# Stick-breaking scores from stacked key parts, half-head value steps, a split last exponential, and a reordered inverse transform

## The reference

```
z = q k^T * 64^-0.5
log_one_minus = where(causal, log_sigmoid(z) - z, 0)
rem = reverse_cumsum(log_one_minus) - log_one_minus
w = where(causal, exp(log_sigmoid(z) + rem), 0)
out = w v
```

## Time and profile before

| | us |
|---|---|
| median of three runs (2299.04 to 2306.05) | 2302.84 |
| profiled execution, its own time | 2304.46 |
| its span in the trace | 2302.7 |
| PE busy | 2166.6 (94%) |
| DVE busy | 1256.4 (55%) |
| ACT busy | 746.9 (32%) |
| POOL busy | 686.1 (30%) |

### The profile page before, as it was taken

The page is one execution under the profiler, slowest core; times in us unless marked ns, Lnnn a source line. Parts: engine busy times, 40 slices in busy tenths (PEclk is TensorE's granted clock), DMA queues, the critical chain, the costliest instruction groups (busy, mean ns, idle before and its releaser), DMA issues. The chain is left out here.

```text
span 2302.7 us, 27418 instructions
## 1 busy us (share of the span) xinstructions
PE 2166.6 (94%) x10821; PEld 1585.2 (69%) x10821; DVE 1256.4 (55%) x2284; ACT 746.9 (32%) x1067; POOL 686.1 (30%) x408
## 2 busy tenths in 40 slices
PE   7859899999999998999999999999999999998988
PEld 6848688888878766778888855436874437885653
DVE  8562389984352066278882032358763563225862
ACT  3422332222142366233232131325651232332210
POOL 6614244445444300344444410011000342441000
PEclk9979899999989999999999989998999979999999
DMA  4032244444423200234443320120002213222102
GB/s 178 7 55 84 72 140 149 141 124 130 131 74 100 83 1 1 82 110 145 148 137 92 92 116 24 55 73 21 2 2 92 92 73 129 92 92 92 74 19 73
DMA packets 51535, 195.49 MB, mean 85 GB/s; under 512 B 9417, under 2 KB 9593, under 8 KB 46191
## 3 DMA queue, kind: packets, MB, share of 16 engines
q1 hardware_dynamic: 37440, 148.53, 20.3%
q0 software_dynamic: 10240, 44.04, 5.5%
q10 hardware_dynamic: 3728, 1.18, 0.3%
HBM read 179.04 MB, written 10.49 MB: 82 GB/s over the span
## 5 line engine op out<-in xcount | busy, mean ns | idle before, releaser
L1474 POOL TENSOR_TENSOR w_lo<-raw,w_hi 128x1024 fp32r<-128x1024 f32 (+1 forms) x216 | 513.7, 2379 | 879.3 <-ACT w_hi L1111 879.2
L586 PE MATMUL psum<-h_hi,w_hi 128*128 128x512 f32 x1216 | 487.9, 401 | 7.7 <-ACT h_hi L1118 5.9
L587 PE MATMUL psum<-h_hi,w_lo 128*128 128x512 f32 x1216 | 480.0, 395 | 0.0
L1111 ACT ACTIVATE w_hi<-raw 128x1024 fp32r<-128x1024 f32 (+1 forms) x216 | 224.9, 1042 | 609.7 <-PE psum L591 399.2
L591 PE MATMUL psum<-h_lo,w_hi 128*128 128x512 f32 x1216 | 303.0, 392 | 0.0
L586 PEld LDWEIGHTS psum<-h_hi,w_hi 128*128 128x128 f32 x1216 | 231.1, 190 | 71.4 <-ACT h_hi L1118 14.4
L591 PEld LDWEIGHTS psum<-h_lo,w_hi 128*128 128x128 f32 x1216 | 230.5, 190 | 48.2
L587 PEld LDWEIGHTS psum<-h_hi,w_lo 128*128 128x128 f32 x1216 | 232.0, 191 | 45.9 <-issue 0.2
L455 PE MATMUL psum<-big,ring 128*128 128x512 f32 x480 | 209.0, 594 | 0.0
L455 PEld LDWEIGHTS psum<-big,ring 128*128 128x128 f32 x480 | 91.0, 191 | 113.8 <-issue 112.7
L633 PE MATMUL psum<-f_hi,w_hi 128*128 128x512 f32 x352 | 137.7, 391 | 0.0
(11 more groups left out here) (374 smaller groups left out, 3326.1 us busy)
## 6 DMA issues: line engine op xcount, KB each, us to landing
raw<-in_ffn_w_up SPq DMA_DIRECT2D x88, 512.0 KB, 3.6
raw<-in_ffn_w_down SPq DMA_DIRECT2D x32, 512.0 KB, 3.6
raw<-in_hy_in SPq DMA_DIRECT2D x32, 512.0 KB, 3.5
ffn_buf<-in_ada_w POOLq DMA_DIRECT2D x20, 512.0 KB, 5.0
sq<-in_ada_w POOLq DMA_DIRECT2D x20, 512.0 KB, 5.0
raw<-in_ssm_w_glu SPq DMA_DIRECT2D x16, 512.0 KB, 3.6
spec<-big SPq DMA_DIRECT2D x8, 1024.0 KB, 3.8
big<-spec POOLq DMA_DIRECT2D x8, 1024.0 KB, 5.1
```

What stands on the lines that cost most here:

```text
L586: pe.matmul(o, hi[:, k, :], h_of(k), start=k == 0, stop=False)
L587: pe.matmul(o, lo[:, k, :], h_of(k), start=False, stop=False)
L1111: act.activation(w_hi[:, (n % 2) * HALF:(n % 2) * HALF + w], raw[:, (n % 4) * HALF:(n % 4) * HALF + w], ACT.Copy).then_inc(S["w_hi"], 1)
L1474: pool.tensor_tensor(w_lo[:, at:at + w], raw[:, (n % 4) * HALF:(n % 4) * HALF + w], w_hi[:, at:at + w].bitcast(F32), ALU.subtract).then_in ...
```

## The change

The keys of a head are now held as a stack: the high part in the head's own 64 partitions, the rest (key minus high part) in the other 64 (`KS`). The queries' high part stands in both halves (`Q_TWICE`), and their rest in `Q_LOW`. A block of scores is one fp32r product over the 128 stacked rows and one fp32r product of the keys' high part with the queries' rest over 64 rows; then the mask as before. ScalarE writes the high parts, VectorE the rests, and GpSimd issues 32 SBUF-to-SBUF DMAs of 128 KB that copy the other halves, between its weight splits; the memsets go. The banks of a head have two keys now, "zA" (blocks 1 to 3) and "zB" (block 0), in this order; the last exponential is in the same two parts, each ahead of the log of that part, and `cum_done` counts three steps per head. `values(t)` is in two steps, block 0 beside head 2t+3 and blocks 1 to 3 beside head 2t+4, both ahead of `cumulate`.

In the Hyena mixer `z_back` runs over the frequency half f outside the four channel blocks and waits for `yw` per half. The last piece, u = 7, is folded, multiplied and summed in two column halves, its fold comes after the sums of u = 6, and `yw` ends at 9.

```diff
-        KZ = bigv(0, 8192).rearrange("p (h t) -> p h t", h=HEADS)
+        KS = f_hi[:, 0:8192].rearrange("p (h t) -> p h t", h=HEADS)
+        K_REST = [v[:, k * L:(k + 1) * L] for v, n in ((f_hi[:, 8192:11264], 6), (f_lo[:, 0:2 * L], 2)) for k in range(n)]
         VT = bigv(8192, 4096).rearrange("p (s n) -> p s n", s=4)
...
+        Q_TWICE = [(HHI, HLO)[h % 2][:, h // 2, :] for h in range(HEADS)]
...
             def scores(h):
...
+                o = z_of(h)
                 if h == 0:
                     pe.wait_ge(S["masks_ready"], 2)
-                    for t in range(8):
-                        pe.wait_ge(*free(("k", t)))
-                        pe.wait_ge(*free(("q", t)))
-                for i in (0, 1, 3, 2):
-                    m = pe.matmul(zblk(o, i), KZ[:, h, i * P:(i + 1) * P], Q[:, h // 2, i * P:L],
-                                  start=i != 3, stop=False, skip_group_check=True)
+                    pe.wait_ge(S["ks_both"], 256)
+                    pe.wait_ge(S["qs_both"], 16 * (HEADS - 2))
+                if h == HEADS - 2:
+                    pe.wait_ge(S["qs_last"], 32)
+                if h % 2 == 0:
+                    pe.wait_ge(*free(("k", h // 2)))
+                    pe.wait_ge(*free(("q", h // 2)))
+                for i in (1, 3, 2, 0):
+                    if i == 1:
+                        take(pe, ("zA", h), bank=3 * (h % 2) + 1, n=2)
+                    if i == 0:
+                        take(pe, ("zB", h), bank=3 * (h % 2))
+                    pe.matmul(zblk(o, i), KS[:, h, i * P:(i + 1) * P], Q_TWICE[h][:, i * P:L], start=i != 3, stop=False,
+                              skip_group_check=True)
+                    m = pe.matmul(zblk(o, i), KS[half(h), h, i * P:(i + 1) * P], Q_LOW[half(h), h // 2, i * P:L],
+                                  start=False, stop=False, skip_group_check=True)
                     m = pe.matmul(zblk(o, i)[:, 0:P], masks[:, 0, :], masks[:, 1, :], start=False, stop=False,
                                   skip_group_check=True)
-                fills(m, key)
+                    if i == 2:
+                        fills(m, ("zA", h))
+                fills(m, ("zB", h))
 
...
                 for ready, sp in ((S["sp_hi"], SPH), (S["sp_lo"], SPL)):
                     pe.wait_ge(ready, 2 * h + 1)
                     for i in (1, 3, 2):
-                        tri(i, sp)
                         later(i, sp)
+                        m = tri(i, sp)
+                m.then_inc(S["cum_done"], 1)
                 pe.wait_ge(S["sp_hi"], 2 * h + 2)
                 later(0, SPH)
                 tri(0, SPH)
-                later(0, SPL)
+                later(0, SPL).then_inc(S["cum_done"], 1)
                 pe.wait_ge(S["sp_lo"], 2 * h + 2)
                 m = pe.matmul(zblk(o, 0), NEGTRI, SPL[:, 0:L], start=False, stop=True, skip_group_check=True)
                 m.then_inc(S["cum_done"], 1)
 
...
-            def values(t):
...
+                o = ps(key) if late else take(pe, key, bank=6 + t % 2)
+                if not late:
+                    for h in (2 * t, 2 * t + 1):
...
+                for i in (1, 2, 3) if late else (0,):
...
                         m = pe.matmul(o[r:r + 64, i * P:L], VT[:, i, h * HD:(h + 1) * HD],
                                       WT[h % 4][:, ZAT[i]:ZAT[i] + L - P * i], start=i == 0, stop=i == 3,
...
+                if late:
+                    fills(m, key)
+
+            for h in range(HEADS + 3):
                 if h < HEADS:
                     scores(h)
+                if h >= 3:
+                    values((h - 3) // 2, h % 2 == 0)
                 if 1 <= h <= HEADS:
                     cumulate(h - 1)
-                if h >= 3 and h % 2:
-                    values((h - 3) // 2)
...
             def z_back(o_, hf):
...
+                keys = [("y", o_, 4 * hf + c) for c in range(4)]
+                for f in range(2):
+                    for c in range(4):
+                        if f == 0:
+                            take(pe, keys[c])
+                        o = ps(keys[c])
+                        if c == 0 or (o_, hf, f, c) == (1, 1, 1, 2):
+                            pe.wait_ge(S["yw"], 2 * (2 * o_ + hf) + f + 1 + c // 2)
+                        for par in range(2):
                             for q, tab in enumerate((INVC, INVS)):
                                 i = pe.matmul(o[:, par * 256:par * 256 + 256], YW[hf][:, f, 2 * q + par, c * P:(c + 1) * P],
-                                              tab[:, f, par * 256:par * 256 + 256], start=f == 0 and q == 0,
-                                              stop=f == 1 and q == 1)
-                    fills(i, key)
+                                              tab[:, f, par * 256:par * 256 + 256], start=f == 0 and q == 0 and par == 0,
+                                              stop=f == 1 and q == 1, skip_group_check=True)
+                        if f:
+                            fills(i, keys[c])
 
...
-                act.wait_ge(S["kz_zero"], t // 2 + 1)
                 act.wait_ge(*full(key))
-                step(act.activation(KZ[0:64, 2 * t, :], ps(key)[0:64, :], ACT.Copy))
-                own()
-                frees(act.activation(KZ[64:128, 2 * t + 1, :], ps(key)[64:128, :], ACT.Copy), key)
+                for h in (2 * t, 2 * t + 1):
+                    act.activation(KS[half(h), h, :], ps(key)[half(h), :], ACT.Copy).then_inc(S["ks_hi"], 1)
...
                 split_hi(HALVES_AT["q"] + t + 2)
-                evac(("q", t), Q[:, t, :], scale=HD ** -0.5)
+                act.wait_ge(*full(("q", t)))
+                for h in (2 * t, 2 * t + 1):
+                    act.activation(Q_TWICE[h][half(h), :], ps(("q", t))[half(h), :], ACT.Copy, scale=HD ** -0.5) \
+                        .then_inc(S["qs_hi"], 1)
...
+                act.wait_ge(*full(("zA", h)))
+                act.wait_ge(*full(("zB", h)))
...
+                own()
+                for q, (lo, hi) in enumerate(SP_PARTS):
+                    if h >= 1:
+                        weights(h - 1, q)
                     act.activation(LN_[b][:, lo:hi], LN_[b][:, lo:hi], ACT.Ln, bias=1.0).then_inc(S["ln_ready"], 1)
...
+            def weights(h, q):
+                act.wait_ge(S["cum_done"], 3 * h + (1, 3)[q])
+                if h >= 4 and q == 0:
                     act.wait_ge(*full(("o", (h - 4) // 2)))
...
+                lo, hi = SP_PARTS[q]
+                z = z_of(h).rearrange("p b n -> p (b n)")[:, lo:hi]
+                frees(act.activation(WT[h % 4][:, lo:hi], z, ACT.Exp), (("zA", "zB")[q], h))
...
+                if t < 8:
+                    split_lo(HALVES_AT["k"] + t + 2)
+                if t:
+                    pool.wait_ge(*free(("k", t - 1)))
+                    for h in (2 * t - 2, 2 * t - 1):
+                        other_half("ks_both", h, KS[:, h, :], K_REST[t - 1])
+            for q in range(7):
+                split_lo(HALVES_AT["v"] + q + 2)
+            for t in range(9):
+                if t < 8:
+                    split_lo(HALVES_AT["q"] + t + 1)
+                if t:
+                    for h in (2 * t - 2, 2 * t - 1):
+                        pool.wait_ge(S["qs_hi"], h + 1)
+                        other_half("qs_both" if t < 8 else "qs_last", h, Q_TWICE[h], Q_TWICE[h])
...
+                for h in (2 * t, 2 * t + 1):
+                    dve.wait_ge(S["ks_hi"], h + 1)
+                    i = TT(K_REST[t][half(h), :], ps(("k", t))[half(h), :], KS[half(h), h, :].bitcast(F32), ALU.subtract)
+                    if h % 2:
+                        frees(i, ("k", t))
+                    else:
+                        step(i)
+                        own()
+            dve.wait_ge(S["ks_both"], 256)
...
+                    i = STT(Q_LOW[half(h), t, :], ps(("q", t))[half(h), :], HD ** -0.5,
+                            Q_TWICE[h][half(h), :].bitcast(F32), ALU.mult, ALU.subtract)
...
                     z_fold(5)
-                after = z_products(u)
-                if u not in (4, 7):
-                    if u != 3:
+                parts = [slice(0, 512)] if u < 7 else [slice(0, 256), slice(256, 512)]
+                for n in parts:
+                    if u == 7:
+                        z_fold(u, n)
+                    after = z_products(u, n)
+                    if u not in (3, 4, 6, 7):
                         z_fold(u + 1)
-                z_sums(u, after)
+                    z_sums(u, after, n)
                 if u == 3:
                     z_fold(4)
...
```

More of the change, by code:

```diff
@@ L714, in cumulate, with values @@
                 m.then_inc(S["cum_done"], 1)
-            def values(t):
-                if t == 0:
+            def values(t, late):
+                if t == 0 and not late:
                     for c in range(2):
@@ L721, in values @@
                 key = ("o", t)
-                o = take(pe, key, bank=6 + t % 2)
-                for h in (2 * t, 2 * t + 1):
```

(44 more changed lines are left out.)

102 lines of the change are left out of this document (41 added, 61 removed).

## The result

The changed kernel takes 2290.47 us (median of four runs, 2288.34 to 2292.03), the kernel before it in the same rounds 2303.52: a ratio of 0.9945, 95% interval 0.9932 to 0.9957. That is 13 us off where 22 were forecast; the time lies in the range. The profiled execution took 2288.34 with a span of 2286.5.

A forecast was written before the change was run, and what follows sets the result against it. The attention loop was taken as bound by TensorE's own list plus a 1.56 us hole in every second head. Loop 18.6 plus Hyena 3.5, about 22 us off 2304.46, gave 2282 us, range 2267 to 2298.

The forecast's parts named there:

- the loop's hole: Attention loop: TensorE's idle 1.56 us in every second head, waiting for ScalarE's last exponential, was forecast to go.
- The list per head: Attention loop: TensorE's work per head, forecast at 6.63 us, or 5.64 plus 9 tile-shape switches.
- the row of another tile shape: Scores: a profiled 33-by-64 product among full ones, showing 0.09 and 0.14 us per switch; 0.11 was taken.
- the third rival: Scores: the array empties at each row-mode switch, 0.35 us each, giving 2315 us; chance 0.06.
- The 13 steps: Attention loop, third head's scores to the last head's: each from 7.69 to 6.63 us, 13.8 us saved.
- The start: Attention loop's beginning: third head's scores no longer wait for all of cumulate and a whole exponential; about 3 us saved.
- The rival of late copies: Before the attention loop: the query DMAs land late, 4.5 us more, giving 2287 us; chance 0.10.
- The tail: Attention's end, last scores to the next projection: from 14.22 to 12.4 us, 1.8 us saved.
- Around the loop: Extra evacuations, VectorE work and DMA issues beside TensorE, and the loop's wait for DMAs: priced at zero.
- a late eighth channel block: Hyena's projection after the last z_back: VectorE is still evacuating, so the eighth channel block costs 0.5 us.
- free switches: Attention loop: tile-shape switches nearly free, 13 x 1.89 us saved there, giving 2271 us; chance 0.20.
- Cancelled: Loop's gain cancelled by switches near 0.22 us or key tiles making TensorE wait, 2298 to 2304 us; chance 0.12.

The follow-up runs named there:

- the kernel over all rows: Changed kernel with the second product of each score block over all 128 rows instead of the head's own 64: 2272.24 us, ratio 0.9866.
- inverse transform late: Changed kernel with the first inverse transform, z_back(0, 0), waiting for both halves of the products again: 2288.38 us, ratio 0.9938.
- values whole: Changed kernel with the values in one step again, behind cumulate in every second head: 2304.03 us, ratio 1.0001.
- the second edit: Changed kernel with the last exponential in one instruction again, ahead of both logs, three banks taken at once: 2349.79 us, ratio 1.0203.
- the start split: Changed kernel with the first scores waiting only for the query copies of heads 0 to 3: 2291.82 us, ratio 0.9941.

## Why the forecast was right, and which terms were not

- The direction and the mechanism held: the loop's hole went, TensorE's list became the bound, ScalarE's exponential in two records frees the banks in time (but for one wait of 0.71 at 813.65). The size did not: 13 us came where 22 were forecast, and the time lies in the range because the range is 31 us wide.
- The list per head was forecast at 6.63 and is 6.96 (13.93 a pair). Scores: 2.48 forecast, 2.86 measured. Of the 0.38, 0.18 is what the sum had wrong without any change of shape (1.60 forecast, 1.78 in the kernel over all rows): the short products, scaled from 512 columns, were 0.37 too cheap and the masks 0.19 too dear. The other 0.20 is eight changes at 0.135 in place of 0.11. Cumulate 2.88 for 2.80; values 1.23 a head with their switches for 1.34. So the row of another tile shape was near for the way in and low for the way out (0.09 and 0.14 there, 0.10 and 0.19 here), and the two mis-sized terms, the switch and the plain scaling by columns, weigh about the same.
- The Trainium skill, "TensorEngine Tiling (Array Packing)", Key Properties, has a mode change drain TensorE. The runs agree that a change costs something, 0.12 to 0.16 us each counted from none; whether the array drains in that time they don't show. The full emptying of 0.35 that the third rival priced did not come.
- The 13 steps gave 8.0 and not 13.8: 807.20 to 898.94 is 91.7, and before it was 99.7, from 805.93 to the last head's scores. These start at 905.66:
```profile
905.66 1.13 PE L682 MATMUL psum<-big 128*128 128x512 f32 x2 [1.33 <-ACT big L1262]
```
The forecast had them at 905.87, and so the steps at 7.69 for 7.67. At 0.33 more a head 4.3 of the 5.8 are explained and 0.3 by this reading; 0.9 is in the first two steps (14.86 for 13.93), with the hole of 0.71 and 3.4 us at the lower clock behind it.
- The start was forecast 3 us shorter and is 2.3 longer: from the last projection product to the third head's scores 18.86 against 16.53. The step that failed is the landing of the copies, taken at 2.2 and 5.4 here, with weights coming in (131 GB/s in the first window above, 62 around the copies of rows 6). That the load is the reason is argued from these two places; no run varies it. The rival of late copies was right in its mechanism; of the 5.3 us between forecast and outcome 2.5 is idle time (4.28 less 1.78), and the rest goes with a clock that fell as the first scores began (at 792.7, and 0.53 over two heads; before the change it fell at 798.9, and 0.76).
- The tail, from the end of the last scores to the projection: 12.73 for 14.41, 1.7 where 1.8 was forecast. In all the attention gave 7.1 where 18.6 was forecast.
- Around the loop nothing was priced and nothing came: 45.00 of 45.00 busy.
- Hyena: 3.5 forecast, 3.5 measured (195.5 to 192.0). The hole moved behind the first `z_back`, the clock fell there (0.66), undoing it gave 1.5 for the 2.1 forecast; the last `z_back` waits 5.43 for banks, forecast 4, and loses 2.8 to the clock, forecast 2. The 0.5 for a late eighth channel block did not come. That the sum is right to a tenth is luck: its misses go both ways.
- 7.1 and 3.5 are 10.6. The profiled pair differs by 16; 4.6 of this lies in the stretch between, which nothing touched, and 1.1 ahead of the attention, where kernels with the same instructions differ by 4. The medians' 13 leaves 2.4, inside what medians of four runs tell.
- The rivals: free switches (2271) would have needed 1.60 for the scores; their time came out only when the changes were taken away. Cancelled (switch near 0.22): the single switch out of the 64-row shape is 0.19, the mean is not.

What stays open: why the holes of the kernel before left its clock at 1.00 and shorter holes beside fp32r products did not. No run here varies the kind of product alone. Nor is it the hole alone: ten of the kernels with the new scores have one of 0.66 to 0.71 before the fourth head's scores (813.65 above), and in three of them, the changed kernel, inverse transform late and values whole, the clock fell about 3 us behind it.

## What to carry to other kernels

Price a short product from a row of its own length, not by columns; and put products of one tile shape together before counting what each saves. Where a start waits for copies, count the landing under the load of that moment and let the first user wait only for its own. A wait moved earlier only moves a hole, and where the hole goes decides what the clock costs.

## What the runs showed of the hardware

- A change between 128-row and 64-row fp32r products costs 0.10 us in and 0.19 us out beside 384 columns, 0.135 on the mean of eight.
- A 128 KB copy between SBUF tiles landed 4.7 to 5.4 us after its issue where weights were loading (775 to 787 us, 131 GB/s), 2.4 to 2.5 for the last two (issued at 790.40 and 791.01), and 2.2 in another place.
- Holes of 0.7 us in every second head stood beside a granted clock of 0.89 over the loop, holes of 1.3 to 1.4 in every head beside 0.77, where the loop without holes has 1.00; the second edit cost 53 us for 19 of idle time.
- The same instructions between attention and Hyena took 1165.4, 1170 or 1174.5 us. In the mixer's first part the two ends look like this, the changed kernel and the one with the start split:
```profile
1800.00:1840.00 40.00, 36.76 (x81) 16.72 (x82) 31.76 (x50) 11.47 (x19) 14.51 (x12) 0.84 0.13 53
```
```profile
1796.47:1836.47 40.00, 38.83 (x70) 17.04 (x71) 26.09 (x40) 10.24 (x17) 14.07 (x12) 0.71 0.10 43
```
From the same instruction on, 81 records at a clock of 0.84 and 70 at 0.71. What decides between them no run here shows.
